# Behind norms 0, 2 and 3: an addition moved on VectorE, statistics and weights moved on ScalarE, and one weight split moved on GpSimd

## The reference, cut to what matters

```python
for l in range(DEPTH):                                   # DEPTH = 2
    x = layer_norm(ALPHA * x + 0.5 * swiglu(x, ffn1_w_in[l], ffn1_w_out[l]), ln1_g[l], ln1_b[l])
    x = layer_norm(ALPHA * x + hybrid_mixer(x, ...), ln2_g[l], ln2_b[l])
    x = layer_norm(ALPHA * x + memory_cross_attn(x, mem, ...), ln3_g[l], ln3_b[l])
    x = layer_norm(ALPHA * x + 0.5 * swiglu(x, ffn2_w_in[l], ffn2_w_out[l]), ln4_g[l], ln4_b[l])

def layer_norm(x, g, b):
    mu = jnp.mean(x, axis=-1, keepdims=True)
    var = jnp.mean(jnp.square(x - mu), axis=-1, keepdims=True)
    return (x - mu) * lax.rsqrt(var + EPS) * g + b
```

## Time and profile before

| | us |
|---|---|
| median of 3 runs | 2215.99 (2215.76 to 2216.14) |
| the profiled execution's own time | 2216.65 |
| its span, first to last instruction | 2214.9 |
| TensorE matmul busy | 2171.3 (98%) |
| VectorE busy | 1119.5 (51%) |
| ScalarE busy | 824.0 (37%) |
| GpSimd busy | 990.5 (45%) |
| granted TensorE clock | 0.997 of full speed |

### The profile page before, as it was taken

How to read it: one execution, slowest core, us unless ns; L and a number is a source line. 1 busy time by engine, 2 the same in 40 slices (tenths; PEclk the granted TensorE clock), 3 DMA queues, 4 the chain that set the end, 5 groups by cost and what they waited for, 6 DMA issues and landing times. The chain is left out here.

```text
span 2214.9 us, 26968 instructions
## 1 busy us (share of the span) xinstructions
PE 2171.3 (98%) x11052; PEld 1814.8 (82%) x11052; DVE 1119.5 (51%) x1222; ACT 824.0 (37%) x1148; POOL 990.5 (45%) x408
## 2 busy tenths in 40 slices
PE   8999999999999999999999999999999999999997
PEld 7888889788778888888888888898786888888886
DVE  4433235987746733323454333369877376333234
ACT  3322224836444522222353222257355344222223
POOL 3444444436443544444354444454265335444442
PEclk9999999999999999999999999999999999999999
DMA  5333322333332233332233333223243222333321
GB/s 179 96 95 95 114 100 62 89 103 105 107 93 67 77 95 96 96 120 92 74 105 95 95 99 117 89 67 86 90 121 113 77 67 80 101 96 95 114 94 49
DMA packets 96043, 210.91 MB, mean 95 GB/s; under 512 B 39344, under 2 KB 52016, under 8 KB 95664
## 3 DMA queue, kind: packets, MB, share of 16 engines
q1 hardware_dynamic: 94944, 208.19, 30.4%
q10 hardware_dynamic: 976, 1.00, 0.1%
HBM read 207.06 MB, written 2.10 MB: 94 GB/s over the span
## 5 line engine op out<-in xcount | busy, mean ns | idle before, releaser
L567 POOL TENSOR_TENSOR w_lo<-raw,w_hi 128x1024 fp32r<-128x1024 f32 (+2 forms) x358 | 930.9, 2602 | 1197.0 <-ACT w_hi L1272 1196.9
L1272 ACT ACTIVATE w_hi<-raw 128x1024 fp32r<-128x1024 f32 (+2 forms) x358 | 401.6, 1122 | 1217.8 <-PE psum L647 1141.1
L641 PE MATMUL psum<-acts_hi,w_hi 128*128 128x512 f32 x1744 | 685.1, 393 | 3.4 <-ACT tmp L1648 3.0
L644 PE MATMUL psum<-acts_lo,w_hi 128*128 128x512 f32 x1744 | 679.8, 390 | 0.0
L647 PE MATMUL psum<-acts_hi,w_lo 128*128 128x512 f32 x1744 | 430.8, 389 | 0.0
L641 PEld LDWEIGHTS psum<-acts_hi,w_hi 128*128 128x128 f32 x1744 | 328.0, 188 | 76.5 <-issue 3.9
L644 PEld LDWEIGHTS psum<-acts_lo,w_hi 128*128 128x128 f32 x1744 | 328.0, 188 | 69.7 <-issue 2.4
L647 PEld LDWEIGHTS psum<-acts_hi,w_lo 128*128 128x128 f32 x1744 | 327.4, 188 | 68.0
L1885 DVE TENSOR_TENSOR work<-work,psum 128x512 f32<-128x512 f32 x85 | 58.5, 688 | 548.8 <-PE psum L647 542.0
L641 PE MATMUL psum<-h_hi,w_hi 128*128 128x512 f32 x616 | 239.6, 389 | 0.0
L644 PE MATMUL psum<-h_lo,w_hi 128*128 128x512 f32 x616 | 239.6, 389 | 0.0
(11 more groups left out here) (300 smaller groups left out, 2484.6 us busy)
## 6 DMA issues: line engine op xcount, KB each, us to landing
raw<-w_in SPq DMA_DIRECT2D x176, 512.0 KB, 3.6
raw<-w_out SPq DMA_DIRECT2D x64, 704.0 KB, 4.0
raw<-w_kv SPq DMA_DIRECT2D x32, 512.0 KB, 3.6
raw<-w_mix SPq DMA_DIRECT2D x26, 512.0 KB, 3.6
raw<-w_q SPq DMA_DIRECT2D x16, 512.0 KB, 3.6
raw<-w_o SPq DMA_DIRECT2D x16, 512.0 KB, 3.6
raw<-w_v SPq DMA_DIRECT2D x4, 768.0 KB, 4.2
raw<-w_mix SPq DMA_DIRECT2D x24, 128.0 KB, 3.3
```

The costliest lines, as they stand in the source:

```text
L567: nc.gpsimd.tensor_tensor(w_lo[:, n % SPLIT, 0:width], raw[:, n % RAW, 0:width], w_hi[:, n % SPLIT, 0:width].bitcast(F32), ALU.subtract).t ...
L641: nc.tensor.matmul(o, hi, b_hi, start=start and k == 0, stop=False)
L644: nc.tensor.matmul(o, hi, b_lo, start=False, stop=False)
L1272: A(w_hi[:, n % SPLIT, 0:width], raw[:, n % RAW, 0:width], ACT.Copy).then_inc(w_hi_made, 1)
```

## The change

There are three edits, all at the five places.

1. VectorE: `added_b` stood at the start of half b, behind all of half a. It now stands within half a, behind the second pair of tiles at norm 2 and behind the third pair at norms 0 and 3.
2. ScalarE: the square of the mean of half b moves ahead of the first two high-part copies of half a, the root ahead of gain and bias of tiles 4 and 5, and the rounding of the third slot's weights from behind `sums_of(0)` to ahead of all of half b.
3. GpSimd: the split of the third slot moves from behind four low parts of half a to behind three.

```diff
@@ after_norm, GpSimd
                 for k in range(0, KT, 2):
                     split_x(x_layer, n, 0, k)
-                split(layer, s + 2)
+                    if k == 4:
+                        split(layer, s + 2)
                 for k in range(0, KT, 2):
                     split_x(x_layer, n, 1, k)
@@ scaled_later, ScalarE
                 w_hi_of(next_s + 1)
+                square_of_mean(layer, n, 1)
                 if n != 2:
                     act.wait_ge(slot_multiplied, next_s)
                 act.drain()
                 copied(0, 0)
                 copied(0, 2)
-                square_of_mean(layer, n, 1)
+                root(layer, n, 1)
                 affines(0, 4)
-                root(layer, n, 1)
                 affines(0, 6)
                 act.drain()
                 copied(0, 4)
                 copied(0, 6)
+                w_hi_of(next_s + 2)
                 for k in range(0, KT, 2):
...
                     if k == 0:
                         sums_of(0)
-                        w_hi_of(next_s + 2)
@@ norm_by_halves, VectorE
                 for h in range(2):
-                    if h:
+                    if h and not later(layer, n):
                         added_b()
...
                     for k in range(4, KT, 2):
+                        if h == 0 and later(layer, n) and k == (4 if n == 2 else 6):
+                            added_b()
                         centered_pair(n, h, k)
```

## The result

The changed kernel takes 2223.94 us (median of 5, 2223.37 to 2225.39) against 2215.99 before (2215.76 to 2216.58): ratio 1.0036, 95% interval 1.0025 to 1.0046. It is slower by 8 us, and the forecast of 2215.4 with its range of 2210.5 to 2218.5 is wrong. The profiled execution, the slowest of the five, took 2225.39 us, its span is 2223.6, and the mean granted clock is 0.993 against 0.997. Two later executions of another kernel, at mean clocks of 0.35 and 0.75, took 8108 and 2710 us and enter no comparison.

A forecast was written before the change was run, and what follows sets the result against it. TensorE was taken as the bound, busy 2171.3 of 2214.9 us, with only its idle time at five places to win. +1.2 (norms 0 and 3) and -1.8 (norm 2) gave -0.6 from 2215.99: 2215.4 us, range 2210.5 to 2218.5.

The forecast's parts named there:

- VectorE's hold: Beside a gap-free GpSimd, one VectorE gain-and-bias instruction passes per GpSimd instruction, 0.15 us behind its end; all 20 held.
- The tie behind norm 2: VectorE's second low part comes at 737.75, GpSimd's second-slot split at 737.81; VectorE taken first, split ends at 740.5.
- The gain at the statistics: Behind norm 2, TensorE comes to the statistics at 736.27 instead of 737.48: 1.21 us gained.
- The trade of two waits for one: Norms 0 and 3: stalls of 1.48 us go, one of about 1.9 comes, +0.4 each; norm 2: gain 0.9.
- The shown waits: TensorE's waits for the last high parts, as the view shows them: 1.7 us behind norms 0 and 3, 2.3 behind norm 2.
- The DMAs and VectorE's delay into the mixer: Behind the places: third slot's DMA about 2.3 us earlier, VectorE 1.6 us late into the mixer; all costed at nothing.
- It has 2 + 8 + 8 matmuls of 0.12 left: 2.15 us, to 393.2: Norm 0: TensorE starts at 391.05 behind the wait for the last high parts and ends 2.15 us later; before, 392.83.
- TensorE from 753.7, 2.15 more: Norm 2: TensorE restarts behind the last high parts and ends at 755.85 against 756.76 before, gain 0.9 us.
- The variance misses the end of the split: Rival, five places: variance held one low part more, 1.3 us each, 6.5 in all: 2221.9 us; chance 0.06.
- VectorE was held a second time: Its rival, not held a second time: low parts bound the pair of slots, 7.6 us won, 2208.4; chance 0.15.
- VectorE kept the tie: Its rival, VectorE loses the tie at norm 2: variance 1.0 us later, two places, +2.0, 2217.4 us; chance 0.15.

The follow-up runs named there:

- rest alone: Changed kernel with the third slot's rounding (ScalarE) and split (GpSimd) put back as before: 2213.42 us, ratio 0.9988.
- filled by half: Changed kernel plus 8 extra TensorE matmuls of 256 columns, sums thrown away, ahead of the last two high parts of half b: 2216.80 us, ratio 1.0002.
- weights alone: Kernel before with only the third slot's weights moved (GpSimd's split, ScalarE's rounding): 2213.97 us, ratio 0.9992.

## Why the prediction was wrong

**What held.** VectorE's hold, one instruction for each of a gap-free GpSimd: all 20 lengthened (1.1 to 1.7 us each), the end at norm 0 exact once the start is allowed for. The tie behind norm 2. The gain at the statistics (rest alone: -1.37 and -1.38 behind norm 2 against the forecast's -1.2). The trade of two waits for one: +0.44 us measured without the half clock against +0.4, and -0.85 behind the first layer's norm 2 (filled by half) against -0.9. The shown waits of 2.0 and 2.3 to 2.6 us were forecast as 1.7 and 2.3, a small miss. The wait of 0.8 us for `sums_of(0)` behind norm 2 was not foreseen, and cost nothing by itself. The DMAs and VectorE's delay into the mixer cost nothing, as assumed: away from the listed places the ledger moves by under 0.4 us in every kernel.

**What failed.** It is the step "It has 2 + 8 + 8 matmuls of 0.12 left: 2.15 us, to 393.2", and its twin behind norm 2, "TensorE from 753.7, 2.15 more". Both took the duration of a matmul from the earlier trace rows, where the clock is full, and carried it behind a pause that the kernel before does not have there. Measured: 3.65 us behind norm 0. At full clock the same 18 matmuls took 2.25 us (393.07 - 390.82 behind norm 0 of the half filled kernel, 1494.38 - 1492.13 in the second profile of the changed one), so 0.1 of the difference is the estimate of 0.12 us for each and 1.4 is the clock. The sum had no term for the clock: the price of half rate behind a new long pause was put at nothing without a reason. The mean clock of 0.997 stood in the table of the profile, and its missing 0.003 lies in stretches that can be looked up: the last 8 us, and one of 3.4 us behind a crowd of short waits at 1712.

**The size, step by step.** From the ledger of the changed kernel: start +0.45, then +2.00, +0.50, +1.88, +1.96 and +0.74 at the five places, and +1.31 at 617, where a stretch appears that the other execution had not. The five places sum to 7.1 us where -0.6 was forecast. At 1.3 to 1.6 us each, five stretches are 6.5 to 8 of these 7.7 us. With the clock kept full by eight extra matmuls the five places sum to -0.1, and that kernel's 2216.80 us lie within the stated range: but for the clock the forecast would have held, some 0.5 us too low. The profiled execution is 1.45 us above the median of the changed kernel; whether that is one stretch more is not shown.

**The rivals.** "The variance misses the end of the split" gave 2221.9, the nearest number, by a mechanism that did not occur: the variance ended at 377.53 + 0.91 = 378.44 us, 377.99 without the late start, as forecast. No rival held a long wait to cost more than it lasts, and an end slower by over 0.2% had a chance of 0.07 in all. VectorE was held a second time, and VectorE kept the tie, so the two others are out as well.

**What stays open.** Which pause brings the half clock. The two profiles of the changed kernel have ten pauses of 2.0 to 2.6 us; behind nine it came, behind one (2.02 us, norm 0 of the second layer) it did not. The two profiles of the kernel with the weights alone have four of 2.3 to 2.6 us; it came behind none. Behind pauses of 1.6 us and less at these places it came in no profile here. But at 617 (five of the twelve profiles) and at 1712 (two of them) it came behind waits of 0.8 to 1.5 us close together, and it comes and goes there in kernels that are alike at that place. So the length of the pause alone does not tell it, and no run here settles what does.

## What to carry to other kernels

Collecting several short waits of TensorE into one long one is not neutral, even where the sum says so: the matmuls behind it can run at half rate for 3.4 us. Where a forecast leaves a pause like those here (2.0 to 2.6 us in a stretch that was dense), give it a term of its own for the clock (some 1.5 us here, with the chance that it comes: 9 of 14 cases over four profiles), and look up the granted clock in a narrow window around the existing pauses before taking a matmul's duration across a new one. And two moves that each win a little can feed the same bound: here it took two steps more, one pair of gain and bias off the engine that was held and the statistics back behind the copies, to win 11 us at the five places. Before a difference of 1 to 2 us is put down to an edit, see whether a stretch at half clock elsewhere has come or gone: one did so at 617 or at 1712 in every comparison here.

## What the runs showed of the hardware that was not expected

- A single pause of 2.0 us in an otherwise dense TensorE was followed by 3.4 us at half clock (window 0.57 for 4 us), at a price of 1.3 to 1.6 us; so it was in 9 of 14 pauses of 2.0 to 2.6 us.
- Adding 40 or 80 matmuls that compute nothing made the kernel 7 us faster than without them.
- The same kernel took 2221.0 and 2225.4 us in its two profiled executions, with its waits the same to 0.01 us behind norm 0; seven stretches at half clock against four account for 4.1 of these 4.4 us, the start for the rest.
- At the start of an execution matmuls of 512 columns come 0.43 us apart instead of 0.23 for 10.2 to 13.2 us, different each time, which by itself shifts everything behind it by up to 1.6 us (start column of the ledger).
- Foretold, and borne out 20 times of 20: VectorE's gain and bias were served between GpSimd's gap-free instructions, one for each, so that two of 0.4 us took 2.4 to 3.0.
